# Moving the second layer's affine of the normed x from GpSimd, inside attention, to VectorE, inside the first output projection

## The reference

```
h = x * (1 + sc_a) + sh_a
proj = h @ w_in[l]                       # q, k, v of three mixers
y = concat(dilated window attention (4 heads), latent attention (4 heads),
           grouped-query attention (8 heads)) @ w_o[l]
x = layer_norm(ALPHA * x + (1 + g_a) * y, ln1_g[l], ln1_b[l])
h = x * (1 + sc_m) + sh_m
y = square(relu(h @ w1[l])) @ w2[l]
x = layer_norm(ALPHA * x + (1 + g_m) * y, ln2_g[l], ln2_b[l])
```

## Time and profile before

| | us |
|---|---|
| median of three runs | 1417.81 |
| the profiled execution | 1415.57 |
| its span in the trace | 1413.7 |
| TensorE (PE) busy | 1319.4 (93%) |
| VectorE (DVE) busy | 989.9 (70%) |
| ScalarE (ACT) busy | 606.2 (43%) |
| GpSimd (POOL) busy | 332.6 (24%) |

### The profile page before, as it was taken

How to read it: one execution, slowest core, us unless ns; L and a number is a source line. 1 busy time by engine, 2 the same in 40 slices (tenths; PEclk the granted TensorE clock), 3 DMA queues, 4 the chain that set the end, 5 groups by cost and what they waited for, 6 DMA issues and landing times.

```text
span 1413.7 us, 19903 instructions
## 1 busy us (share of the span) xinstructions
PE 1319.4 (93%) x6888; PEld 1120.2 (79%) x6888; DVE 989.9 (70%) x1676; ACT 606.2 (43%) x1260; POOL 332.6 (24%) x427
## 2 busy tenths in 40 slices
PE   4998999799999999999999899889999999999995
PEld 2897777688988888888879877668888888888884
DVE  6658779884688656655775877989377964545577
ACT  0446478771532222222254547778343222222221
POOL 0013057550415000000030404956030700000005
PEclk9999989999999999999999999989999999999998
DMA  8864500103344443443236461010225423333322
GB/s 293 294 210 147 181 14 1 40 1 95 101 162 153 153 141 108 156 153 97 82 109 243 134 218 70 1 32 9 77 73 179 157 91 97 97 96 96 99 94 96
DMA packets 88165, 164.54 MB, mean 116 GB/s; under 512 B 8024, under 2 KB 18648, under 8 KB 88080
## 3 DMA queue, kind: packets, MB, share of 16 engines
q1 hardware_dynamic: 87408, 161.08, 34.8%
q10 hardware_dynamic: 672, 2.36, 0.5%
HBM read 159.21 MB, written 4.19 MB: 116 GB/s over the span
## 4 chain that ended last, share of the span: by engine, by line
PE 66%; DVE 14%; DMA 7%; ACT 5%; POOL 5%; issue 3%; SPq 0%; POOLq 0%; DVEq 0%; ACTq 0%
PE bank L1505 21%; PE bank L1507 20%; PE bank L1506 20%; DMA slab_raw<-in_w_in 4%; DVE pt_lo L1178 2%; DVE ada_sum L938 1%; DMA band<-bias_rows 1%; PE bank L1722 1%; DVE smax L1165 1%; DMA ada_w<-in_w_ada 1%; PE bank L1536 1%; POOL prob L536 1%; ACT slab_hi L606 1%; DVE k_lo L1139 1%; DVE prob L1161 1%
## 5 line engine op out<-in xcount | busy, mean ns | idle before, releaser
L1505 PE MATMUL bank<-hT_hi,slab_hi 128*128 128x512 f32 (+1 forms) x640 | 236.0, 369 | 2.4 <-ACT kB L755 2.4
L1507 PE MATMUL bank<-hT_hi,slab_lo 128*128 128x512 f32 (+1 forms) x640 | 235.4, 368 | 0.0
L1506 PE MATMUL bank<-hT_lo,slab_hi 128*128 128x512 f32 (+1 forms) x640 | 235.4, 368 | 0.0
L1280 DVE TENSOR_TENSOR slab_lo<-slab_raw,slab_hi 128x512 fp32r<-128x512 f32 x240 | 172.3, 770 | 67.3 <-ACT slab_hi L880 44.2
L1505 PE MATMUL bank<-slab_hi,h_hi 128*128 128x512 f32 x512 | 201.5, 394 | 0.4 <-DVE slab_lo L1280 0.4
L1507 PE MATMUL bank<-slab_hi,h_lo 128*128 128x512 f32 x512 | 199.4, 389 | 0.0
L1506 PE MATMUL bank<-slab_lo,h_hi 128*128 128x512 f32 x512 | 199.3, 389 | 0.0
L1505 PE MATMUL bank<-slab_hi,hT_hi 128*128 128x384 f32 (+3 forms) x448 | 153.8, 343 | 10.3 <-DVE slab_lo L982 3.7
L982 DVE TENSOR_TENSOR slab_lo<-slab_raw,slab_hi 128x512 fp32r<-128x512 f32 (+3 forms) x144 | 83.3, 587 | 106.5 <-ACT slab_hi L606 106.3
L498 POOL TENSOR_SCALAR mv<-mv 128x1 f32<-128x1 f32 x16 | 5.5, 346 | 642.8 <-DVE mv L1226 642.1
L1507 PE MATMUL bank<-slab_hi,hT_lo 128*128 128x384 f32 (+3 forms) x448 | 151.3, 338 | 0.0
(11 more groups left out here) (199 smaller groups left out, 2571.3 us busy)
## 6 DMA issues: line engine op xcount, KB each, us to landing
slab_raw<-in_w SPq DMA_DIRECT2D x256, 256.0 KB, 2.7
ada_w<-in_w_ada SPq DMA_DIRECT2D x48, 1024.0 KB, 6.0
slab_raw<-in_w_in SPq DMA_DIRECT2D x48, 192.0 KB, 5.1
slab_raw<-in_w_o SPq DMA_DIRECT2D x32, 256.0 KB, 2.6
slab_raw<-in_w_in SPq DMA_DIRECT2D x16, 256.0 KB, 3.8
band<-bias_rows SPq DMA_DIRECT2D x8, 448.0 KB, 3.1
slab_raw<-in_w_in SPq DMA_DIRECT2D x16, 144.0 KB, 4.6
X<-in_x SPq DMA_DIRECT2D x1, 2048.0 KB, 9.7
```

Of the source, the lines that this page charges most:

```text
L1280: dve.tensor_tensor(slab_lo[:, slot, :], slab_raw[:, slot, :], f32(slab_hi[:, slot, :]), ALU.subtract).then_inc(slab_lo_done, 1)
L1505: pe.matmul(dst, a_hi, w_hi, start=first, stop=False)
L1506: pe.matmul(dst, a_hi, w_lo, start=False, stop=False)
L1507: return pe.matmul(dst, a_lo, w_hi, start=False, stop=last)
```

## The change

In layer 1 POOL no longer touches x during attention and makes the reciprocal of every unit itself, as in layer 0. DVE's reciprocals in attention go, and so does ACT's wait for the affine. The two rows now go to one tile `lnxrow`, which lies over memory of `qkA`. SP issues their loads behind the whole loop over the 64 projection slabs, after a wait for `head_ready` 13 of the layer (the last reader of `qkA` there) and ahead of the wait for `y_ready`. DVE applies the affine in the loop that splits the slabs of wo1: after the split of slab 56+k it multiplies and adds one half tile of x, and waits for its own multiplication in between. Before the first of these it waits for both loads. The residual waits for the last.

```diff
-AFFINE_FROM = 8
-def affine_unit(l, u):
-    return l > 0 and AFFINE_FROM <= u < AFFINE_FROM + 4 * TT
...
+        lnxrow = over("lnxrow", [P, 2, D], 0)
...
                     if i == 55:
                         wait_apart(sp, slab_free, l * SLABS + RING + 8 * (A_QK + 1))
-                        if l > 0:
-                            sp.dma_start(lnx_g[:, :], ...).then_inc(lnx_in, 16)
-                            sp.dma_start(lnx_b[:, :], ...).then_inc(lnx_in, 16)
...
+                if l > 0:
+                    wait_apart(sp, head_ready, l * NH + 13)
+                    for j in range(2):
+                        sp.dma_start(lnxrow[:, j, :], t_in["ln_rows"][l, j:j + 1, :].broadcast_to([P, D])
+                                     ).then_inc(lnx_in, 16)
                 wait_apart(sp, y_ready, l * NH + NH)
...
                 for u in range(UNITS):
                     p = prob[:, u % 4, :]
-                    if affine_unit(l, u):
-                        pool.wait_ge(summed, sums_by_dve(l, u) + 1)
-                    else:
-                        pool.wait_ge(exped, l * UNITS + u + 1)
-                        after(step(pool.tensor_tensor(smax[:, u % 4, 2:3], ..., mone[:, 0:1], ALU.pow)))
+                    pool.wait_ge(exped, l * UNITS + u + 1)
+                    after(step(pool.tensor_tensor(smax[:, u % 4, 2:3], ..., mone[:, 0:1], ALU.pow)))
                     pool.tensor_scalar(p, p, smax[:, u % 4, 2:3], 1.0, ALU.mult, ALU.mult).then_inc(normed, 1)
-                    if affine_unit(l, u):
-                        n = u - AFFINE_FROM
-                        affine_part(n // 4, n % 4, lnx_g, lnx_b)
...
-                        if (kt, hf) == (2, 0):
-                            act.wait_ge(x_ready, l * 8 + 4)
...
-                    if 0 <= u < UNITS and affine_unit(l, u):
-                        dve.wait_ge(exped, l * UNITS + u + 1)
-                        if u >= 4:
-                            dve.wait_ge(normed, l * UNITS + u - 3)
-                        dve.reciprocal(smax[:, u % 4, 2:3], smax[:, u % 4, 1:2]).then_inc(summed, 1)
...
+                def affine_of_x(t, j):
+                    xs = X[:, t, 512 * j:512 * j + 512]
+                    step(dve.tensor_tensor(xs, xs, lnxrow[:, 0, 512 * j:512 * j + 512], ALU.mult))
+                    settle()
+                    step(dve.tensor_tensor(xs, xs, lnxrow[:, 1, 512 * j:512 * j + 512], ALU.add))
+
                 for k in range(8):
                     split(56 + k, 512)
-                dve.wait_ge(x_ready, l * 8 + 4)
+                    if l > 0:
+                        dve.wait_ge(lnx_in, 32)
+                        affine_of_x(k // 2, k % 2)
+                settle()
                 dve.wait_ge(slab_free, l * SLABS + RING + 56)
```

More of the change, by code:

```diff
@@ L84 @@
 ATT_STEPS = UNITS + 8
-AFFINE_FROM = 8
-def affine_unit(l, u):
-    return l > 0 and AFFINE_FROM <= u < AFFINE_FROM + 4 * TT
-def sums_by_dve(l, u):
-    return sum(affine_unit(m, v) for m in range(l) for v in range(UNITS)) + sum(affine_unit(l, v) for v in range(u))
 OUT_AT = [(4 + h // 2, h % 2) if m == "C" else (h // 2, h % 2) if m == "A" else (2 + h // 2, h % 2)
@@ L215, in trunk @@
         lnrow = over("lnrow", [P, 2, D], 34816)
-        lnx_g = nc.alloc_sbuf_tensor_at("lnx_g", [P, D], F32, offset=hT_at + 4 * 2 * S)
-        lnx_b = nc.alloc_sbuf_tensor_at("lnx_b", [P, D], F32, offset=hT_at + 4 * KT * S + 4 * 2 * S)
+        lnxrow = over("lnxrow", [P, 2, D], 0)
         h2_hi = over("h2_hi", [P, 2, 4, S], 0, F32R)
@@ L294, in trunk @@
             sem, ("k_hi_done", "head_hi", "head_ready", "v_hi_done", "v_ready"))
-        scored, maxed, exped, summed, normed, transposed, pt_hi_done, pt_ready, pv_done, y_hi_done, y_ready = map(
-            sem, ("scored", "maxed", "exped", "summed", "normed", "transposed", "pt_hi_done", "pt_ready",
+        scored, maxed, exped, normed, transposed, pt_hi_done, pt_ready, pv_done, y_hi_done, y_ready = map(
+            sem, ("scored", "maxed", "exped", "normed", "transposed", "pt_hi_done", "pt_ready",
                   "pv_done", "y_hi_done", "y_ready"))
@@ L439, in _ @@
                 w2_slabs(GROUPS - 1, l * SLABS + (SLABS - 8 + 1), 0)
-            sp.wait_ge(x_ready, DEPTH * 8)
+            sp.wait_ge(x_ready, DEPTH * TT)
             sp.dma_start(lnrow[:, 0, :], t_in["ln_last"][0:1, :].broadcast_to([P, D])).then_inc(ln_in, 16)
@@ L526, in _ @@
                     inv_sqrt(rms[:, n % TT, j:j + 1], msq[:, n % TT, j:j + 1], 1, brstd_done)
-                if l == 0:
-                    pool.sem_inc(x_ready, TT)
                 for u in range(UNITS):
                     p = prob[:, u % 4, :]
-                    if affine_unit(l, u):
-                        pool.wait_ge(summed, sums_by_dve(l, u) + 1)
-                    else:
-                        pool.wait_ge(exped, l * UNITS + u + 1)
-                        after(step(pool.tensor_tensor(smax[:, u % 4, 2:3], smax[:, u % 4, 1:2], mone[:, 0:1], ALU.pow)))
-                    pool.tensor_scalar(p, p, smax[:, u % 4, 2:3], 1.0, ALU.mult, ALU.mult).then_inc(normed, 1)
-                    if l > 0 and u == AFFINE_FROM:
-                        pool.wait_ge(bank_ready, l * B_LAYER + 16)
-                        pool.wait_ge(lnx_in, 32)
-                    if affine_unit(l, u):
-                        n = u - AFFINE_FROM
-                        affine_part(n // 4, n % 4, lnx_g, lnx_b)
+                    pool.wait_ge(exped, l * UNITS + u + 1)
+                    after(step(pool.tensor_tensor(smax[:, u % 4, 2:3], smax[:, u % 4, 1:2], mone[:, 0:1], ALU.pow)))
+                    pool.tensor_scalar(p, p, smax[:, u % 4, 2:3], 1.0, ALU.mult, ALU.mult).then_inc(normed, 1)
                 normalise(0)
@@ L1166, in _ @@
                                               ).then_inc(maxed, 1)
-                    u = s - 1
-                    if 0 <= u < UNITS and affine_unit(l, u):
-                        dve.wait_ge(exped, l * UNITS + u + 1)
-                        if u >= 4:
-                            dve.wait_ge(normed, l * UNITS + u - 3)
-                        dve.reciprocal(smax[:, u % 4, 2:3], smax[:, u % 4, 1:2]).then_inc(summed, 1)
                     u = s - LO_LAG
@@ L1369, in _ @@
                     split_at(k, base_at + (PRE + 16 + k + 1))
-                dve.wait_ge(x_ready, l * 8 + 8)
+                dve.wait_ge(x_ready, (l + 1) * TT)
                 dve.wait_ge(evac_act, relu_base + 5 * LATE)
```

## The result

The changed kernel took 1430.86 us (median of four runs, 1430.0 to 1432.08) against 1417.01 before: a ratio of 1.010, 95% interval 1.0082 to 1.0117. It is slower, by 14 to 17 us. The prediction was 1432, range 1425 to 1438. The two profiled executions lie 14.8 us apart (1430.41 and 1415.57), their spans 14.9.

The account below looks back on a forecast made before the run. PE, busy 93% of the span, was taken to bound the kernel, with POOL bounding 16 attention units and DVE the output projection's chain. -4.0 + 17.0 + 1.9 = +14.9 us gave 1430.5 to 1432.7, predicted 1432, range 1427 to 1438 (also given as 1425 to 1438).

Parts of the forecast that it names:

- Attention, -4.0: Layer 1's attention, units 8 to 32: runs at layer 0's pace, 45.81 us for 49.79, saving 4.0 us.
- The loads behind slab 63: SP's queue: row loads wait for wo0's end, take lnrow's places, and the second lands 5.2 us after issue, at 1026.8.
- the rival of four loads sharing the engines: SP's queue: the new loads and lnrow's share engines, landing 7.6 us after issue; +17.3, 1435.1 us; chance 0.12.
- The chain of DVE behind the wait, 15.1 us: Output projection: 16 operations and seven splits take 15.1 us; the first residual starts 17.0 us later.
- PE's gaps: Output projection: PE waits 7.0 us after wo1's first slab and 7.8 us at the transposes, broken by one transpose.
- The clock, +1.9: PE behind the transposes' gap: half clock for about 4 us costs 1.9 us; ends 0 and 2.3.
- The sum, +14.9: Whole kernel: -4.0 for attention, +17.0 for the residual's delay, +1.9 for the clock, making +14.9 us.
- the residuals' chain is hidden: Rival, output projection: only PE's waits for slabs count; +6.6 us, or 1424.4; chance 0.07.
- the loads come in time: Rival, output projection: loads issued before wo1's slabs let operations fit DVE's gaps; -2.6 us, or 1415.2; chance 0.04.
- landing plus 15.2 us: Output projection: the first residual's delay is the rows' landing time + 15.2 - 1025.04, which is 4.0 at 1013.8.
- The clock did not hold unaided: Rival, PE behind the gap: the clock holds at full speed; +13.0 us, or 1430.8; chance 0.15.
- Attention gained no more than layer 0 shows: Rival, layer 1's attention: a gain over four times what layer 0 shows brings the sum to zero; chance 0.03.

Follow-up runs that it names:

- the spare matmuls: The changed kernel with 28 spare matmuls of 128x512 in PE's gap before layer 1's transposes; 1432.99 us, again 1430.17 us.
- the first series: The changed kernel's first measurement against the kernel before: 1430.86 us against 1417.01, ratio 1.010.
- the second: The unaltered changed kernel measured again against the kernel before: 1432.44 us against 1415.31, ratio 1.0125.
- splits first: The changed kernel with all eight splits ahead of the wait and the 16 affine operations; 1429.42 us, again 1428.99 us.
- the loads were early: The changed kernel with the two row loads issued before the slabs of wo1, behind the bands; 1414.62 us, ratio 0.9977.
- slab 59: The changed kernel with the two row loads issued behind slab 59 in place of slab 63; 1422.58 us, ratio 1.0051.

## Why the prediction was right

* **Attention, -4.0.** Measured -4.07 (A). Layer 0 as a model of layer 1 was right to 0.1 us.
* **The loads behind slab 63.** As read from the code's order. They landed 4.6 and 5.4 us after issue; I took 5.2 for the second. lnrow's loads behind them landed at 6.1 and 6.9, against 4.4 and 5.2 before. Over all profiles lnrow's second load took 5.2 to 5.8 us where its pair stood alone behind the slabs and 6.9 to 7.7 behind the new pair, whose own second load took 5.4 to 6.1 there. The two in front nearly kept their price and those behind paid, so the rival of four loads sharing the engines (7.6 for the two in front) is out. The Trainium skill (DMA: Bandwidth & Descriptors, HWDGE ordering) says that each DMA engine takes the descriptors of a ring in ring order; the trace agrees, with 5.4 us for the load in front and 6.9 for the one behind.
* **The chain of DVE behind the wait, 15.1 us.** From 1022.93 to 1037.89 it is 14.96. With the wait, the first residual came 12.85 us later while SP's last slab came 4.04 earlier, 16.9 in all against the 17.0 of the sum. The operations ran at 0.61 and 0.72, the rows' spacing.
* **PE's gaps.** The first was 7.07 (forecast 7.0). The waits at each further slab came only twice, 0.21 and 0.30, where I had 0.6 each time: at half clock PE takes longer for a slab than DVE. The second gap was 7.0 in place of 7.8; from the last slab to the remaining 15 transposes it is 7.5 us (1046.46 to 1053.92), with one transpose in it. Neither error enters the sum, since the transposes' time follows DVE's chain: 1053.92, where the forecast is 1058.0 - 4.04 = 1053.96.
* **The clock, +1.9.** C grew by 1.74 and 2.44 in two profiles, and the spare matmuls took all of it away. The second value is just above my end of 2.3, which named no row; half of the 4 us that I read is 2.0, not 1.9.
* **The sum, +14.9.** The stretches give -4.07 + 16.83 + 1.74 + 0.31 = +14.8 in the pair of profiles; the median of the first series moved by 13.9, of the second by 17.1. The mechanism and its terms are shown by the stretches; that the forecast of 1432 lies within 1.2 us of both medians of the changed kernel is in part luck, since the two series differ by 3 us in what the change adds.
* **The rivals.** That the residuals' chain is hidden is refuted by "splits first". That the loads come in time did not happen, but its 1415.2 is what was measured once the loads were early (1414.6), so its mechanism was right and only the queue's order decided against it. The prediction's point, landing plus 15.2 us, held at slab 59. The clock did not hold unaided in either profile of the changed kernel. Attention gained no more than layer 0 shows.

## What to carry to other kernels

In this kernel a load placed at the end of a queue of loads inherited the wait of the last of them, the end of a whole matmul stage; read the position in the issuing queue before the cost of the operations. Work put on DVE, idle for 30% of the span, was free only where it came in its gaps and ahead of the last split: the same 16 operations, with the wait for their rows, cost 0, 1.3 or 17 us by place. And when such a stall is shortened, ask where the waiting engine will wait next: behind slab 59 the gap at the second slab was gone, and the 7.0 us at the transposes still cost 2.4 us by the clock.

## What had not been expected of the hardware

POOL's affine had also stretched VectorE's work. These are the last two splits of q on DVE (64x512, both operands in SBUF) inside the affine's units before, with POOL's operations around the first:

```profile
901.99 1.28 POOL L490 TENSOR_TENSOR X<-X,lnx_b 128x512 f32<-128x512 f32 x1
902.19 1.63 DVE L1146 TENSOR_TENSOR q_hi<-qC,q_hi 64x512 fp32r<-64x512 f32 x1
903.25 1.13 POOL L536 TENSOR_SCALAR prob<-prob,smax 128x512 f32<-128x512 f32 x1
...
910.06 1.93 DVE L1146 TENSOR_TENSOR q_hi<-qC,q_hi 64x512 fp32r<-64x512 f32 x1
```

The later of the two after the change:

```profile
907.93 0.72 DVE L1120 TENSOR_TENSOR q_hi<-qC,q_hi 64x512 fp32r<-64x512 f32 x1
```

Before, the last four of its kind in those units took 0.92, 1.20, 1.63 and 1.93 us; after, all take 0.69 to 0.74. Each of the four ended 0.54 to 0.59 us behind the end of one of POOL's operations that it overlapped: the first one shown at 903.82, POOL's at 903.27. The Trainium skill (SBUF — State Buffer, SBUF: two separate sides) says that an operation of DVE with two operands in SBUF and one of GpSimd that reads SBUF exclude each other for a whole instruction. The trace agrees, in both directions: each of the four got done only once POOL's had ended, and POOL's product behind the first one shown took 1.13 us in place of 0.70 and ended 0.56 us behind DVE's. It shows in a row as a longer operation, not as idle time.

With the affine at every second unit only one of these splits was stretched, to 1.01 us, and yet 1.7 us of A's price stayed. So the stretched splits are not what that run failed to win back; they may be part of what it won. There POOL's own additions and multiplications were the longer ones, 24.65 us for the 16 where they took 21.91 before. No run separates these effects from POOL's rate.
